# Five edits to a two-layer FP32 transformer kernel on one core: the squares a weight half later, a block-masked bias, an earlier third chunk, fewer unused matmuls, and the head norm on column groups

## The chip, the cores and the metric

The kernel runs on one core of one Trainium2 chip. The metric is the device time of one execution in microseconds. One execution was also recorded by the hardware profiler; all rows of a trace in this document come from such an execution, and its times count from the start of its span.

The core's engines are named as the trace names them: PE is the matrix engine (PEld is its weight load, which overlaps), DVE the vector engine, ACT the scalar engine, POOL the GpSimd engine, SP the engine that here only starts transfers. Each engine runs its own instructions in order and waits on semaphores for the others.

## The reference

Two transformer blocks follow each other on 256 tokens of width 1024, all in FP32. Cut to what matters here:

```python
def first_block(x, ...):
    proj = rms_norm(x, attn_norm_g) @ w_in
    y_moba = attention(rope(q), rope(k), v)          # 8 heads of 64, causal
    og = gla_attention(gq, gk, gv, log_a)            # 4 heads, 128 values each
    og = og * lax.rsqrt(jnp.mean(og * og, axis=-1, keepdims=True) + EPS) * gla_norm_g   # the head norm
    y_gla = og * silu(gr)
    x = x + concat(y_moba, y_gla) @ w_out
    h = causal_dwconv(rms_norm(x, ffn_norm_g) @ w_ffn_up, conv_w, conv_b)   # width 3
    x = x + (silu(h_gate) * h_val) @ w_ffn_down
    return rms_norm(x, final_norm_g)

def second_block(x, c, ...):
    (sh1, sc1, g1, sh2, sc2, g2, sh3, sc3, g3) = split(silu(c) @ w_ada + b_ada)
    x = x + 0.5 * g1 * swiglu(modulate(rmsnorm(x), sh1, sc1), ffn1_w_in, ffn1_w_out)
    z = modulate(rmsnorm(x), sh2, sc2) @ w_in        # latents, chunk attention q k v, two gates
    y_a = mla_attention(...) @ w_branch_a            # normalised latents, then w_uq and w_ukv
    y_b = chunk_attention(..., rel_bias) @ w_branch_b   # scores + rel_bias, masked by chunks of 64
    x = x + g2 * ((sigmoid(gate_a) * y_a + sigmoid(gate_b) * y_b) @ w_out)
    x = x + 0.5 * g3 * swiglu(modulate(rmsnorm(x), sh3, sc3), ffn2_w_in, ffn2_w_out)
    return rmsnorm(x, final_norm)
```

The feed-forward widths are 2816, so each up projection has 22 pairs of 128 columns and each down projection 22 tiles of contraction.

## The kernel before, in words

Activations stand with features on the 128 partitions and the 256 tokens along the free axis. Every product of an activation with a weight is done in three passes of FP32R matmuls (`three`, L393 to L395): weight-high by activation-high, weight-high by activation-low, weight-low by activation-high.

The weights come as 282 **halves** of 128 x 1024 (512 KB). A half is loaded by SP into one of four slots of `raw`, ACT copies it to `w_hi` (`hi`, L881), DVE subtracts to `w_lo` (`lo`, L1285), and PE uses it in 24 matmuls. Two halves are one **chunk**. SP may load half h when `w_lo` of half h-4 is made; ACT may write `w_hi` of half h when PE has used half h-4; PE waits for `lo_ready` before each half. All engines' orders are written out by hand.

The stages in order: input projection (chunks 0 to 11), its attention and gated linear attention between them, the output projection (12 to 15), the convolved up projection (16 to 37, halves 32 to 75), its down projection (halves 76 to 97), the second block's first up projection (98 to 141) and down projection (142 to 163), its input projection and latents (from half 164), eight gate chunks with the attentions between them, the branches, the output projection, the last up projection (halves 216 to 259) and the last down projection (260 to 281).

At a stage's first pair of chunks (`first_two`) PE takes the first halves of both chunks in turn, feature tile by feature tile, as the normalised tiles arrive. Before it, where the input isn't taken raw, `keep_clock` issues `IDLE_SPREAD` matmuls of 128 x 384 in FP32 whose output nobody reads; the trace shows two rows for each such matmul.

In `ffn_down`, output tile o is done by PE every 22 groups of three matmuls. DVE adds it to `X` (`ffn_resid`, L1389 or L1391) at the half that `OUT_AT` names, ACT squares it right then (`square`, L889; after the first block `gain_square`, L895, too), and POOL adds the squares up (L343, L351). PE sums them over partitions early in the next `first_two` (`sums`, at feature tile `sums_at`), since the next stage takes `X` unnormalised and scales its output.

In the convolved up projection ACT takes a chunk from PSUM with the middle tap (L993), then makes the `w_hi` of two chunks on; DVE adds the two other taps (L1546, L1549), frees the bank, makes the `w_lo`, and multiplies. While that goes on DVE also takes 72 dot products of `ada_w` with `silu(c)` (`ada`, L1576) in slots of its own.

The head norm (in the loop over g at g == 3) sums the squares of four heads by 8 matmuls with one moving column (L728), takes root and reciprocal of 128 x 8 values and spreads them back by 8 matmuls of 128 columns (L484). The bias of the chunk attention is loaded by POOL in one transfer (L373) and POOL adds the mask to it in eight instructions (L377), once the latents' root is taken (`lat_sd`).

## Time and profile before

| | |
|---|---|
| median of 3 runs | 881.8 us (881.03, 881.8, 885.49) |
| the profiled execution's own time | 885.38 us |
| its span in the trace | 883.6 us |
| PE busy | 864.9 us (98%), 7342 matmul rows |
| DVE busy | 702.6 us (80%) |
| ACT busy | 474.2 us (54%) |
| POOL busy | 88.7 us (10%) |
| weight matmuls, 128 x 256 and 128 x 258 | 6726 of the matmul rows, by the groups of L393 to L395, L467 to L469 and L796 to L798 |

Some 1.8 us of the profiled execution lie outside its span. A matmul's busy time in the trace (276 to 281 ns for 256 columns) is longer than the step from one to the next, since they are pipelined; so "98% busy" says that PE seldom waits, and not how fast it goes. The step is read from a count of matmuls over a stretch. An idle time in brackets behind a row is what the engine stood idle before that row, and what ended it.

### The profile page before, as it was taken

How to read it: one execution, taken by the hardware profiler on the slowest of the kernel's cores; microseconds unless marked ns; L12 is line 12 of the kernel's file. 1: busy time of each engine (PE TensorE's matmuls, PEld its weight loads, DVE VectorE, ACT ScalarE, POOL GpSimd, SP SyncE). 2: the span in 40 equal slices, each digit the busy share in tenths (PEclk: the TensorE clock that was granted, in tenths of full speed). 3: DMA queues.
4: the chain of work that ended last, by engine and by line, in shares of the span. 5: the costliest groups of instructions: out<-in, count | busy, mean ns of one | idle time of the engine just before them, and what ended most of it. 6: DMA issues, size and time to landing. Idle time of an engine off the chain costs nothing.

```text
span 883.6 us, 19377 instructions
## 1 busy us (share of the span) xinstructions
PE 864.9 (98%) x7342; PEld 838.6 (95%) x7342; DVE 702.6 (80%) x1109; ACT 474.2 (54%) x747; POOL 88.7 (10%) x135
## 2 busy tenths in 40 slices
PE   8999999999999999999999999999999999999996
PEld 7988998999999999999999999888899999999996
DVE  4998755889998788888887877888989998766552
ACT  4846665655555458444443467555645754444452
POOL 1022002000000321000001100300010100000010
PEclk8999999999999999999999999999999999999999
DMA  7543336556667985688888866655577568556651
GB/s 269 172 163 96 121 123 259 164 180 207 210 213 263 330 301 180 220 291 293 286 293 282 300 224 241 213 191 178 205 250 258 207 196 287 196 199 192 211 172 48
DMA packets 53335, 191.80 MB, mean 217 GB/s; under 512 B 5920, under 2 KB 6432, under 8 KB 53152
## 3 DMA queue, kind: packets, MB, share of 16 engines
q1 hardware_dynamic: 41760, 149.96, 50.9%
q0 software_dynamic: 10656, 39.33, 13.1%
q10 hardware_dynamic: 864, 1.73, 0.6%
q8 instruction: 39, 0.64, 0.3%
q14 instruction: 16, 0.13, 0.0%
HBM read 189.95 MB, written 1.05 MB: 216 GB/s over the span
## 4 chain that ended last, share of the span: by engine, by line
PE 84%; DVE 11%; ACT 3%; issue 1%; DMA 1%; SPq 0%; POOL 0%; DVEq 0%; ACTq 0%
PE ps L393 25%; PE ps L394 24%; PE ps L395 24%; DVE w_lo L1285 5%; DVE ada_raw L1576 2%; ACT w_hi L881 1%; PE ps L467 1%; PE ps L532 1%; PE ps L469 1%; PE ps L468 1%; PE ps L589 1%; DMA raw<-w 1%; PE ps L563 1%; PE ps L400 1%; PE ps L484 1%
## 5 line engine op out<-in xcount | busy, mean ns | idle before, releaser
L1285 DVE TENSOR_TENSOR w_lo<-raw,w_hi 128x1024 fp32r<-128x1024 f32 (+1 forms) x282 | 341.2, 1226 | 86.9 <-ACT w_hi L881 86.5
L393 PE MATMUL ps<-xh,w_hi 128*128 128x256 f32 x1296 | 364.6, 281 | 1.6 <-DVE w_lo L1285 1.6
L394 PE MATMUL ps<-xl,w_hi 128*128 128x256 f32 x1296 | 360.4, 278 | 0.0
L395 PE MATMUL ps<-xh,w_lo 128*128 128x256 f32 x1296 | 360.4, 278 | 0.0
L881 ACT ACTIVATE w_hi<-raw 128x1024 fp32r<-128x1024 f32 (+1 forms) x282 | 287.0, 1047 | 45.6 <-PE ps L395 30.0
L393 PEld LDWEIGHTS ps<-xh,w_hi 128*128 128x128 f32 x1296 | 244.1, 188 | 5.2 <-issue 3.4
L395 PEld LDWEIGHTS ps<-xh,w_lo 128*128 128x128 f32 x1296 | 244.9, 189 | 0.0
L394 PEld LDWEIGHTS ps<-xl,w_hi 128*128 128x128 f32 x1296 | 243.5, 188 | 0.9 <-issue 0.8
L393 PE MATMUL ps<-act_hi,w_hi 128*128 128x256 f32 x528 | 146.4, 277 | 1.5 <-DVE w_lo L1285 1.5
L395 PE MATMUL ps<-act_hi,w_lo 128*128 128x256 f32 x528 | 146.0, 277 | 0.0
L394 PE MATMUL ps<-act_lo,w_hi 128*128 128x256 f32 x528 | 146.0, 277 | 0.0
L393 PEld LDWEIGHTS ps<-act_hi,w_hi 128*128 128x128 f32 x528 | 99.1, 188 | 2.1 <-DVE w_lo L1285 1.9
L394 PEld LDWEIGHTS ps<-act_lo,w_hi 128*128 128x128 f32 x528 | 99.3, 188 | 0.0
L395 PEld LDWEIGHTS ps<-act_hi,w_lo 128*128 128x128 f32 x528 | 99.2, 188 | 0.0
L1576 DVE SCALAR_TENSOR_TENSOR ada_raw<-ada_raw,cact 128x1024 f32<-128x1024 f32 x72 | 87.5, 1218 | 0.0
L334 POOL DMA_DIRECT2D ada_raw<-ada_w x72 | 38.5, 535 | 452.1 <-DVE ada_raw L1576 452.1
L1000 ACT ACTIVATE sg<-ps 128x256 f32<-128x256 f32 x36 | 13.8, 384 | 115.2 <-PE ps L395 115.2
L889 ACT ACTIVATE xn<-X 128x256 f32<-128x256 f32 (+1 forms) x37 | 17.7, 479 | 84.0 <-DVE X L1391 50.3
L393 PE MATMUL ps<-xr_h,w_hi 128*128 128x258 f32 x176 | 50.6, 287 | 3.0 <-DVE w_lo L1285 3.0
L394 PE MATMUL ps<-xr_l,w_hi 128*128 128x258 f32 x176 | 50.0, 284 | 0.0
L993 ACT ACTIVATE cv<-ps,cols 128x256 f32<-128x256 f32 x44 | 22.5, 562 | 51.3 <-PE ps L395 51.3
L395 PE MATMUL ps<-xr_h,w_lo 128*128 128x258 f32 x176 | 49.7, 282 | 0.0
(261 smaller groups left out, 1144.5 us busy)
## 6 DMA issues: line engine op xcount, KB each, us to landing
raw<-w SPq DMA_DIRECT2D x282, 512.0 KB, 4.3
ada_raw<-ada_w POOLq DMA_DIRECT2D x72, 512.0 KB, 4.7
X<-x_in SPq DMA_DIRECT2D x4, 256.0 KB, 5.7
bm<-bias_in POOLq DMA_DIRECT2D x1, 1024.0 KB, 6.2
out<-X SPq DMA_DIRECT2D x4, 256.0 KB, 2.4
tab<-tab_in ACTq DMA_DIRECT2D x1, 640.0 KB, 4.4
gmask<-gmask_in ACTq DMA_DIRECT2D x1, 512.0 KB, 5.3
cact<-c_in POOLq DMA_DIRECT2D x1, 512.0 KB, 6.0
```

Source lines behind the costliest of these rows:

```text
L334: pool.dma_start(ada_raw[:, n % 4, :], ada_w[n, :, :]).then_inc(ada_landed[n % 4], 16)
L393: pe.matmul(o, lh, rh, start=start, stop=False, skip_group_check=True)
L394: pe.matmul(o, lh, rl, start=False, stop=False, skip_group_check=True)
L395: return pe.matmul(o, ll, rh, start=False, stop=stop, skip_group_check=True)
L400: pe.matmul(ps[:, bank, 0:3 * P], mean[:, 0, :], mean[:, :, :].rearrange("p a n -> p (a n)"), start=True, stop=True)
L467: pe.matmul(o, ah[:, kc, a], w_hi[:, slot(h), wcol], start=first and f == 0, stop=False, skip_group_check=True)
L881: f(w_hi[:, slot(h), 0:n], raw[:, slot(h), 0:n], ACT.Copy).then_inc(hi_ready, 1)
L889: f(xn[:, k:k + n, :], X[:, k:k + n, :], ACT.Square).then_inc(sq_done, n)
L993: ins = f(cv[:, v, t2, 0:S], ps[:, b, t2 * S:t2 * S + S], ACT.Identity, scale=wcol, bias=bcol)
L1000: f(sg[:, v, :], ps[:, b, 0:S], ACT.Silu).then_inc(sg_done, 1)
L1285: v.tensor_tensor(w_lo[:, slot(h), 0:n], raw[:, slot(h), 0:n], w_hi[:, slot(h), 0:n].bitcast(F32), ALU.subtract).then_inc(lo_ready, 1)
L1576: v.scalar_tensor_tensor(out=ada_raw[:, k, :], in0=ada_raw[:, k, :], scalar=1.0, in1=cact[:, :], op0=ALU.mult, op1=ALU.mult, accum_out=mod ...
```

## The change

- `IDLE_SPREAD` goes from 2 to 1 (the two `first_two` that don't take their input raw: the kernel's start and the convolved up projection).
- Head norm: the sums of squares are 4 matmuls with 32 stationary columns of 1/128 each, to 32 partitions per head (column groups), 256 moving columns; root and reciprocal are now of 128 x 256; the spread is 4 matmuls of 256 columns with a matrix `g_pick` that picks a head's row.
- The norm before the convolved up projection sums tile 6 first, then 0 and 1 (which wait for POOL's sum), then 7.
- Convolved up projection: the high and low parts of the third chunk's weights are made before the first chunk is taken from PSUM.
- `ffn_down`: each square stands one weight half later in ACT's order. DVE's order is as it was.
- Bias: the masked quarter is filled with -1e30 by a memset, the rest loaded by two transfers; the eight additions go. DVE waits for the transfers at the chunk attention's masks.
- Last up projection: POOL adds the squares only when the low parts of the first two halves are made, and PE sums them after the fourth feature tile, not the third.

```diff
@@ -28,7 +28,7 @@
 IDLE = 6
-IDLE_SPREAD = 2
+IDLE_SPREAD = 1
 NEXT = [(0, 1), (1, 1), (2, 2), (4, 2), (6, 2)]
@@ -152,7 +152,7 @@
                     ("pt1", [P, 2, 768], F32), ("st1", [P, 2, 3, 4], F32),
-                    ("g_rstd", [P, S], F32),
+                    ("g_rstd", [P, S], F32), ("g_pick", [P, 4, P], F32),
                     ("posi", [P, S], I32)])
@@ -172,7 +172,7 @@
         bank_free = [sem("bank0_free"), sem("bank1_free")]
-        mean_ready, consts_ready, pool_zero = sem("mean_ready"), sem("consts_ready"), sem("pool_zero")
+        pick_ready, mean_ready, consts_ready, pool_zero = sem("pick_ready"), sem("mean_ready"), sem("consts_ready"), sem("pool_zero")
         rstd_spread, out6_full = sem("rstd_spread"), sem("out6_full")
@@ -317,6 +317,11 @@
             pool.memset(b1["AT1"][:, :, :], 0.0).then_inc(pool_zero, 1)
+            own.mark(pool.memset(b1["g_pick"][:, :, :], 0.0))
+            own.wait()
+            for h in range(4):
+                pool.memset(b1["g_pick"][32 * h:32 * h + 1, h, :], 1.0).then_inc(pick_ready, 1)
+            pool.wait_ge(pick_ready, 4)
@@ -370,14 +375,12 @@
             pool.wait_ge(half_used, 2 * C_LAT)
-            pool.dma_start(b2["bm"][:, :, :], bias_in).then_inc(bias_landed, 16)
-            pool.wait_ge(lat_sd, 1)
-            pool.wait_ge(bias_landed, 16)
-            for h in range(8):
-                ins = pool.tensor_tensor(b2["bm"][:, h, :], b2["bm"][:, h, :], table("chunked", S), ALU.add)
-            ins.then_inc(bm_ready, 1)
+            pool.memset(b2["bm"][0:64, :, P + 64:S], NEG).then_inc(bm_ready, 1)
+            pool.dma_start(b2["bm"][0:64, :, 0:P + 64], bias_in[0:64, :, 0:P + 64]).then_inc(bias_landed, 16)
+            pool.dma_start(b2["bm"][64:P, :, :], bias_in[64:P, :, :]).then_inc(bias_landed, 16)
             for n in range(49, 68):
                 load_ada(n)
+            pool.wait_ge(lo_ready, 2 * C_UP[2] + 2)
             for k in (2, 4, 6):
@@ -502,10 +505,11 @@
-                pe.wait_ge(sq_sum, added)
                 for j, k in enumerate(tiles_left):
...
                         pe.wait_ge(sq_done, KC * q + k + 1)
+                    else:
+                        pe.wait_ge(sq_sum, added)
                     m = token_sums(k, j == 0, j == len(tiles_left) - 1)
@@ -592,7 +596,7 @@
                 raw_in = f > 0
-                first_two(c0, m_x, sums=sums, sums_at=f, shifted=raw_in)
+                first_two(c0, m_x, sums=sums, sums_at=2 * f - 1, shifted=raw_in)
                 n = 2
@@ -723,10 +727,9 @@
                     for h in range(4):
-                        pe.wait_ge(go_sq, 2)
-                        for t in range(2):
-                            m = pe.matmul(ps[:, 2, 2 * h + t:2 * h + t + 1], b1["g_sd"][:, h, t * P:t * P + P], mean[:, 2, 0:1],
-                                          start=h == 0 and t == 0, stop=True, skip_group_check=True)
+                        pe.wait_ge(go_sq, h // 2 + 1)
+                        m = pe.matmul(ps[32 * h:32 * h + 32, 2, 0:S], mean[:, 2, 0:32], b1["g_sd"][:, h, :], start=True, stop=True,
+                                      skip_group_check=True)
                     m.then_inc(go_ss, 1)
@@ -736,17 +739,17 @@
+                    pe.wait_ge(pick_ready, 4)
                     pe.wait_ge(go_rstd, 1)
...
                     for h in range(4):
-                        for t in range(2):
-                            o = (h % 2) * S + t * P
-                            m = spread(ps[:, 2 - 2 * (h // 2), o:o + P], b1["g_rstd"][:, 2 * h + t:2 * h + t + 1], h % 2 == 0 and t == 0)
+                        m = pe.matmul(ps[:, 2 - 2 * (h // 2), (h % 2) * S:(h % 2) * S + S], b1["g_pick"][:, h, :], b1["g_rstd"][:, :],
+                                      start=h % 2 == 0, stop=True, skip_group_check=True)
                         if h % 2:
...
             mix_ends(C_OUT1, b1["yh1"], b1["yl1"])
-            norm_tokens(1, 1, 2, (0, 1, 6, 7))
+            norm_tokens(1, 1, 2, (6, 0, 1, 7))
@@ -992,7 +995,8 @@
                     ins.then_inc(cv_base, 1)
-                    hi(c + 2, i=i)
+                    if j:
+                        hi(c + 2, i=i)
                     act.wait_ge(cv_gate, n)
@@ -1008,6 +1012,7 @@
+                hi(c0 + 2)
                 for j in range(2):
@@ -1034,12 +1039,12 @@
                     hi(c0 + p // 2, halves=(p % 2,))
-                    if p in OUT_AT:
-                        square(q, OUT_AT[p])
+                    if p - 1 in OUT_AT:
+                        square(q, OUT_AT[p - 1])
                         if fi == 0:
-                            gain_square(OUT_AT[p])
-                    if last and p in OUT_AT:
-                        final_gain(OUT_AT[p])
+                            gain_square(OUT_AT[p - 1])
+                        if last:
+                            final_gain(OUT_AT[p - 1])
                     if not last and p >= 17:
@@ -1130,7 +1135,7 @@
                     act.wait_ge(go_ss, 1)
-                    f(b1["g_rstd"][:, 0:8], ps[:, 2, 0:8], ACT.Sqrt, bias=epsc[:, 0:1]).then_inc(go_sd, 1)
+                    f(b1["g_rstd"][:, :], ps[:, 2, 0:S], ACT.Sqrt, bias=epsc[:, 0:1]).then_inc(go_sd, 1)
                 att_yh(g, yh1, g)
@@ -1548,11 +1553,13 @@
                         ins.then_inc(cv_gate if t2 == 0 else bank_free[b], 1)
-                    lo(c + 2, i=i, halves=(0,))
+                    if j:
+                        lo(c + 2, i=i, halves=(0,))
                     dve.wait_ge(bank_free[b], u // 2 + 1 + i)
...
                     v.tensor_tensor(av[:, vv, :], sg[:, vv, :], cv[:, vv, 1, 0:S], ALU.mult).then_inc(cv_own, 1)
-                    lo(c + 2, i=i, halves=(1,))
+                    if j:
+                        lo(c + 2, i=i, halves=(1,))
                     dve.wait_ge(cv_own, 3 * (j + 1) + 6 * i)
@@ -1578,6 +1585,7 @@
+                lo(c0 + 2)
                 for j in range(2):
@@ -1733,7 +1741,7 @@
                     dve.wait_ge(go_sd, 1)
-                    v.reciprocal(b1["g_rstd"][:, 0:8], b1["g_rstd"][:, 0:8]).then_inc(go_rstd, 1)
+                    v.reciprocal(b1["g_rstd"][:, :], b1["g_rstd"][:, :]).then_inc(go_rstd, 1)
                 att_y(g, yh1, yl1, g)
@@ -1857,6 +1865,7 @@
                     dve.wait_ge(bm_ready, 1)
+                    dve.wait_ge(bias_landed, 32)
                     att_mask(g, b2["sm2"], b2["st2"], 0.125, lambda a, b_: b2["bm"][:, h:h + 2, a:b_])
             mask2(4)
```

How instructions move, three places. Lines of the changed kernel are 3 and more further down: its L884 is `hi` (L881 before), L892 the square (L889), L898 the gain square (L895), L996 and L1001 are L993 and L997.

ACT from the end of the norm into the convolved up projection, before (`cact` belongs to the ada products, `cv` is the chunk taken from PSUM, `sg` its gate):

```order
L1160 ACTIVATE cact<-cact 128x1024
L993 ACTIVATE cv<-ps,cols 128x256 x2
L881 ACTIVATE w_hi<-raw 128x1024 x2
L997 ACTIVATE sg<-cv 128x256
L993 ACTIVATE cv<-ps,cols 128x256 x2
L881 ACTIVATE w_hi<-raw 128x1024 x2
```

and after:

```order
L1165 ACTIVATE cact<-cact 128x1024
L884 ACTIVATE w_hi<-raw 128x1024 x2
L996 ACTIVATE cv<-ps,cols 128x256 x2
L1001 ACTIVATE sg<-cv 128x256
L996 ACTIVATE cv<-ps,cols 128x256 x2
L884 ACTIVATE w_hi<-raw 128x1024 x2
```

The two halves of the third chunk stand ahead of the first chunk's `cv`; DVE's two `w_lo` move in the same way.

ACT in the middle of the first block's down projection, before (each `xn<-X` is a square, which waits for DVE's addition to `X`):

```order
L881 ACTIVATE w_hi<-raw 128x1024 x3
L889 ACTIVATE xn<-X 128x256
L895 ACTIVATE gain_sq<-X,cols 128x256
L881 ACTIVATE w_hi<-raw 128x1024
L907 ACT_TABLE_LOAD
L907 ACTIVATE epsc<-epsc 128x1
L881 ACTIVATE w_hi<-raw 128x1024
L889 ACTIVATE xn<-X 128x256
L895 ACTIVATE gain_sq<-X,cols 128x256
```

and after:

```order
L884 ACTIVATE w_hi<-raw 128x1024 x3
L892 ACTIVATE xn<-X 128x256
L898 ACTIVATE gain_sq<-X,cols 128x256
L910 ACT_TABLE_LOAD
L910 ACTIVATE epsc<-epsc 128x1
L884 ACTIVATE w_hi<-raw 128x1024 x2
L892 ACTIVATE xn<-X 128x256
L898 ACTIVATE gain_sq<-X,cols 128x256
```

The half that stood behind each square now stands ahead of it.

POOL around the bias (`bm`), before (the first `xn` row is the second block's sum of squares, the last one that of the last norm):

```order
L343 TENSOR_TENSOR xn<-xn 128x256 x2
L373 DMA bm<-bias_in 128x2048
L377 TENSOR_TENSOR bm<-bm,tab 128x256 x8
L334 DMA ada_raw<-ada_w 128x1024 x19
L343 TENSOR_TENSOR xn<-xn 128x512 x3
```

and after:

```order
L348 TENSOR_TENSOR xn<-xn 128x256 x2
L378 MEMSET bm 64x8x64
L379 DMA bm<-bias_in 64x8x192
L380 DMA bm<-bias_in 64x2048
L339 DMA ada_raw<-ada_w 128x1024 x19
L348 TENSOR_TENSOR xn<-xn 128x512 x3
```

The eight additions are gone, and the loads behind them no longer wait for `lat_sd`.

## Rows read from the trace of the kernel before

**Rows 1.** The chain that ended last, share of the span by engine.
```profile
PE 84%; DVE 11%; ACT 3%; issue 1%; DMA 1%; SPq 0%; POOL 0%; DVEq 0%; ACTq 0%
```

**Rows 2.** PE's waits, whole run: waiting <- waited for: us in total, times, longest.
```profile
PE ps L393 <- DVE w_lo L1285: 6.1, 7, 1.4
```

**Rows 3.** Busy time and counts by stretch: span, busy (x) per engine, PEclk, DMA, GB/s.
```profile
160.00:270.00 110.00, 110.00 (x936) 110.00 (x936) 99.43 (x185) 62.26 (x97) 2.11 (x4) 1.00 0.65 204
365.00:475.00 110.00, 110.00 (x973) 110.00 (x973) 93.26 (x141) 45.03 (x58) 11.09 (x21) 1.00 0.84 283
```

**Rows 4.** Timeline at the convolution's third chunk: start, us, engine, line, out<-in [idle before].
```profile
156.15 0.86 DVE L1549 SCALAR_TENSOR_TENSOR cv<-ps,cols,cv 128x254 f32<-128x254 f32 x2
...
156.93 1.22 DVE L1285 TENSOR_TENSOR w_lo<-raw,w_hi 128x1024 fp32r<-128x1024 f32 x1
...
158.20 0.39 PE L393 MATMUL ps<-xh,w_hi 128*128 128x256 f32 x1 [1.21 <-DVE w_lo L1285]
```

**Rows 5.** Timeline in the first down projection, output tile 3.
```profile
307.47 0.42 DVE L1389 TENSOR_TENSOR X<-ps,X 128x256 f32<-128x256 f32 x1
...
308.42 0.74 POOL L343 TENSOR_TENSOR xn<-xn 128x256 f32<-128x256 f32 x1 [2.51 <-ACT xn L889]
...
308.64 2.94 ACT L881 ACTIVATE w_hi<-raw 128x1024 fp32r<-128x1024 f32 x3
...
309.72 1.23 DVE L1285 TENSOR_TENSOR w_lo<-raw,w_hi 128x1024 fp32r<-128x1024 f32 x1 [1.84 <-ACT w_hi L881]
```

**Rows 6.** PE's timeline, the matmul that ends each wait in or behind the down projections.
```profile
311.00 0.38 PE L393 MATMUL ps<-act_hi,w_hi 128*128 128x256 f32 x1 [0.94 <-DVE w_lo L1285]
...
333.79 0.36 PE L393 MATMUL ps<-xr_h,w_hi 128*128 128x258 f32 x1 [0.74 <-DVE w_lo L1285]
...
494.65 0.38 PE L393 MATMUL ps<-act_hi,w_hi 128*128 128x256 f32 x1 [0.59 <-DVE w_lo L1285]
...
518.12 0.36 PE L393 MATMUL ps<-xr_h,w_hi 128*128 128x258 f32 x1 [0.85 <-DVE w_lo L1285]
```

**Rows 7.** Timeline at the latents: POOL's mask additions, DVE, and PE's first matmul behind.
```profile
552.58 6.18 POOL L377 TENSOR_TENSOR bm<-bm,tab 128x256 f32<-128x256 f32 x8 [14.87 <-ACT l_sd L1203]
...
555.91 2.25 DVE L1820 SCALAR_TENSOR_TENSOR lat<-lat,cols,l_sd 128x256 f32<-128x256 f32 x3
558.08 1.76 DVE L1285 TENSOR_TENSOR w_lo<-raw,w_hi 128x1024 fp32r<-128x1024 f32 x1
...
561.94 0.35 PE L393 MATMUL ps<-cqh,w_hi 128*128 128x256 f32 x1 [1.28 <-issue]
```

**Rows 8.** Timeline ahead of the last up projection.
```profile
690.23 1.49 POOL L343 TENSOR_TENSOR xn<-xn 128x512 f32<-128x512 f32 x1 [7.81 <-ACT xn L889]
...
690.49 2.32 DVE L1285 TENSOR_TENSOR w_lo<-raw,w_hi 128x1024 fp32r<-128x1024 f32 x1
...
693.07 0.36 PE L393 MATMUL ps<-xr_h,w_hi 128*128 128x258 f32 x1 [1.37 <-DVE w_lo L1285]
```

**Rows 9.** Busy time in that up projection's raw chunks, columns as in rows 3.
```profile
699.00:718.00 19.00, 19.00 (x160) 19.00 (x160) 18.13 (x25) 16.63 (x26) 0.00 (x0) 1.00 0.47 152
```

**Rows 10.** Timeline at the norm before the convolved up projection.
```profile
143.32 2.77 PE L400 MATMUL ps<-mean 128*128 128x384 f32 x4
...
144.53 0.43 DVE L1317 TENSOR_TENSOR xl<-xn,xh 128x256 fp32r<-128x256 f32 x1
```

**Rows 11.** The stretch of those matmuls, columns as in rows 3.
```profile
142.60:145.90 3.30, 3.30 (x9) 2.09 (x9) 2.25 (x6) 1.45 (x4) 0.13 (x1) 0.50 0.79 288
```

**Rows 12.** Timeline at the head norm, and one output copied out behind it.
```profile
112.37 1.84 PE L728 MATMUL ps<-mean,g_sd 128*128 128x1 f32 x16
...
115.49 0.42 DVE L1489 TENSOR_TENSOR yl<-ps,yh 128x256 fp32r<-128x256 f32 x1 [0.74 <-ACT yh L971]
```

**Rows 13.** Groups by shape: four concurrent 32-column tiles, and a reciprocal of 128 x 256.
```profile
L670 PE MATMUL ps<-xn,w_glr 128*32 128x256 f32 x16 | 1.1, 385 | 0.0
L1290 DVE RECIPROCAL rstd_x<-sd 128x256 f32<-128x256 f32 x1 | 1.7, 1746 | 0.0
```

## The prediction

> **What bounds the kernel now.** I read the chain that ended last first: PE holds 84% of it and DVE 11% [rows 1]. So PE sets the end, and a change is worth what it takes from PE's waits, from PE's work, or from the step between its matmuls. The second view is who waited for whom: PE's first matmul of a half waited 7 times for `w_lo`, 6.1 us in all [rows 2]. The third is a count of matmuls over a stretch, because a busy PE need not be a fast one. In the convolved up projection 936 matmuls started in 110 us, in the second block's up projection 973 [rows 3]: a step of 117.5 ns against 113.1 ns, both at full granted clock and both without a wait. I call them the long and the short step. The change doesn't name them, but a wait removed may change which one follows. The last view is the timeline at each wait, to see what was late there.
>
> An idle time in a row counts from a matmul's modelled end, and a matmul lasts 0.28 us where the step is 0.12 us; so a wait costs its idle time plus about 0.16 us.
>
> **The third chunk's weights first.** PE stood idle 1.21 us for the `w_lo` of the third chunk, 1.37 us lost, because DVE made it (start 156.93) behind the first chunk's taps [rows 4]. Both copies now stand ahead of the first chunk's evacuation, on ACT and on DVE. What is late next is the bank: the third chunk writes where the first stood, and DVE's last tap, which frees it, ends at 156.15 + 0.86 = 157.01. PE would come at 158.20 - 1.37 = 156.83 and waits some 0.2 us for the bank. I take 1.15 us. Nothing else is behind the moved copies but the evacuation, which waits for PE's end of the first chunk anyway.
>
> **The square one half later.** At output tile 3 of the first down projection DVE adds to X at 307.47, ACT squares, squares with the gain, and only then starts the next `w_hi` (308.64); DVE idles 1.84 us for it [rows 5], and PE then idles 0.94 us: 1.10 us lost [rows 6]. The high part could have been made at once, since its raw half had long landed and its slot was free. DVE gains 1.84 us per output tile. But POOL's two additions (0.74 us each, one in rows 5) fell into that idle time, and now fall on busy DVE. Rows 8 show what that may cost: an addition of 1.49 us beside a `w_lo` that took 2.32 us where others take 1.23 us [rows 5]. So the collision costs DVE between nothing and POOL's whole 1.48 us; I take the latter, a net 0.36 us per tile. Four tiles (0 to 3) stand before the wait, 1.4 us, which is more than the 1.10 us that was missing: this wait goes. Behind the down projection PE loses 0.74 + 0.16 = 0.90 us in the same way [rows 6]; there the sums of the last tile follow close behind, and I take 0.75 us. The second block's down projection has the same two waits, 0.75 and 1.01 us [rows 6], and only one addition per tile: 1.75 us. Together 3.6 us; from 2.0 (the collisions take back the waits in the middle) to 3.8.
>
> The Trainium skill ("SBUF — State Buffer", Who interferes with whom) says that a DVE instruction with two SBUF inputs and a GpSimd instruction that reads SBUF block each other for the whole instruction. Rows 8 agree, 2.32 us against 1.23 us. By that rule the upper price above is the one to take.
>
> **The bias without additions.** POOL's eight additions run from 552.58 for 6.18 us. In that time DVE's three instructions on the latents took 2.25 us, where two of this kind take 0.86 us [rows 4], so three 1.3 us; and the `w_lo` behind took 1.76 us [rows 7] against 1.23 us. That is 0.95 + 0.53 = 1.5 us on DVE ahead of PE's first matmul on them, which stood idle 1.28 us, 1.44 us lost [rows 7]. With the additions gone the whole wait goes, 1.4 us; if DVE's slowness had another source, nothing. The transfers are one more, on POOL's queue, and their data is wanted 40 us later.
>
> **The last up projection.** PE idled 1.37 us for that 2.32 us `w_lo` [rows 8]. POOL now waits for it, so it takes 1.23 us and PE starts 1.1 us earlier. But POOL's three additions start at 691.7, not at 690.23: their 4.5 us now lie wholly on DVE's X and weight parts, and DVE comes out of them up to 1.0 us later than now. PE's sums also stand a feature tile later. Behind them DVE is busy 18.13 of 19 us [rows 9], so it can't catch up, and PE, which is 1.1 us earlier, meets it. I keep 0.3 us of 1.1; the bounds are -0.3 and 1.1.
>
> **Norm, fewer unused matmuls, head norm.** Before the convolved up projection four rows of unused matmuls begin at 143.32 and take 0.64 us each, at half clock (0.50, rows 11), so they end at 145.88; the first tile of `xl` is ready at 144.96 [rows 10]. With two rows PE can start at 145.0, 0.88 us earlier. The new order of the sums saves PE some 0.27 us of waiting for POOL. Head norm: the sums took 1.84 us [rows 12]; the gate's 16 rows in four column groups take 1.1 us [rows 13], so 8 rows 0.55 us and a bit, 1.1 us saved. The reciprocal now takes 1.75 us [rows 13], where one of 8 columns was short; it delays the `yl` behind it, which began at 115.49 [rows 12], by nothing in clock time but against a PE that is 1.1 us earlier, so PE waits 0.7 us. I take 0.4 us (bounds -0.5 and 1.1). At the kernel's start I take 0.2 us of what the norm gives, since DVE paces what follows. That is 0.2 + 0.4 + 0.27 + 0.88 = 1.75 us; but real matmuls that start at 144.1 run at 1.2 GHz until the clock rises at about 146, so half of it is lost. I take 0.8 us.
>
> **The sum.** 1.15 + 3.6 + 1.4 + 0.3 + 0.8 = 7.25 us, rounded to 7.3. Against the profiled execution's own 885.4 us (span 883.6 and 1.8 outside) that is 878.1. Now the step: in the convolved up projection some 1,010 matmuls ran behind the wait at 158.20, and each took 4.5 ns more than the short step [rows 3], 4.5 us in all. The three unprofiled runs are 881.0, 881.8 and 885.5: two of them 4 us shorter than the profiled one, the third like it. I read that as this stretch at one step or the other. The median of before is then one with the short step, and so is my forecast: 881.8 - 7.3 = 874.5 us. A half per cent is 4.4 us and about what a measurement of this kernel can tell from no change; the line for faster is 877.4.
>
> **The rivals.**
> - *The long step stays in that stretch.* The 0.2 us wait for the bank starts PE anew there, as the longer wait did, and which step follows a wait differs from one to the next: after 311.00 and 494.65 [rows 6] PE went on fast, after 158.20 slowly. For it: the profiled run. Against it: two of three other runs. Time: 885.4 - 7.3 = 878.1, with smaller gains 879.
> - *DVE gives it back.* The collisions cost more than the waits did in both down projections, and the last up projection gives nothing. Then 3.6 becomes 1.0 or so and 0.3 becomes 0: 881.8 - 7.3 + 2.9 = 877.4, say 878. For it: DVE is at 99.43 of 110 us in one up projection [rows 3]. Against it: in the down projections it idles 1.84 us per tile.
> - *The clock stays low.* The unused matmuls stand where PE has just been at 0.50 [rows 11]. With half of them gone the clock may rise later. If it stayed low as long again as in that row, 3.3 us would hold only 1.65 us of work, and so at each of the two places: 874.5 + 2 to 3 = 877. The Trainium skill ("TensorE: Matmul & The Clock Gate", What's actually happening) says that activity releases the throttle, which speaks for keeping them. The trace agrees in that the rise comes after these matmuls. Against it: real matmuls take their place 0.4 us later.
> - *Slower.* The short step is lost where PE has it now. The stretches from 337 to 494 and from 698 to 875 hold some 1,370 and 1,550 matmuls at 113.1 ns; at 117.5 ns they cost 6.1 and 7.0 us. If the stalls removed before them leave PE in the long step there, the time is 885.4 - 7.3 + 13.1 = 891. It decides from about 1,650 such matmuls on (7.3 us / 4.4 ns). Against it: both stretches begin with matmuls of 258 columns, after which it was the short step each time.
>
> **How the numbers follow.** Forecast 874.5 with the short step: 0.53. Long step, 878.1 to 879: 0.22. DVE gives it back, 878: 0.13. Low clock, 877: 0.07. Slower, 891, or something like it: 0.05. Faster than 877.4 are 0.95 of the first, 0.3 of the second, 0.4 of the third and 0.6 of the fourth, 0.66; slower than 886.2 are 0.04; the rest is 0.30. The forecast's own terms are uncertain by +-2 us, 872 to 877. The range takes in the second and third cases with their errors: 871.5 to 880.5.
>
> **What would show it.** In the profile after: PE's waits for `w_lo` fall from 7 to 2 or fewer. The wait near 157 is 0.3 us or less and names a tap of DVE or nothing. No row of a `w_hi` behind a square has DVE waiting 1.8 us. A POOL addition stands beside a `w_lo` or an ada product of 1.9 us or more in the first down projection. The three latent instructions take 1.3 us and the wait at 561 is gone. In the last up projection the `w_lo` that took 2.32 us takes 1.2, and PE waits somewhere from 700 to 717 for DVE. Counts over 110 us in the convolved up projection say 973 or 936. The forecast is wrong if these counts rise and the time doesn't fall, or if the waits go and come back elsewhere on PE in the same size.

## The result and the profile after

The changed kernel took 878.5 us (median of 20 runs, 871.0 to 884.3) where the kernel before took 881.8 us (20 runs, 879.9 to 885.5): a ratio of 0.9941, interval 0.9921 to 0.996. The ratio compares means and leaves out the 884.3 us run as a slow one (877.3 for 882.4 us); by the medians it is 0.9963. The median is inside the predicted range and 4 us above the predicted 874.5 us. The spread is the news: 13 us, where the kernel before has 6. The profiled execution took 871.0 us (span 869.2), 14.4 us less than the profiled one of before.

The chain that ended last, answering to [rows 1], and PE's waits in the changed kernel, answering to [rows 2] (waiting <- waited for: us in total, times, longest):

```profile
PE 88%; DVE 8%; ACT 1%; issue 1%; DMA 1%; SPq 0%; DVEq 0%; ACTq 0%
```
```profile
PE ps L396 <- DVE w_lo L1290: 0.9, 2, 0.5
...
PE ps L396 <- DVE xl L1357: 0.7, 1, 0.7
...
PE ps L396 <- DVE xl L1322: 0.6, 2, 0.3
PE ps L396 <- DVE act_lo L1575: 0.4, 1, 0.4
PE ps L396 <- DVE yl L1494: 0.3, 1, 0.3
PE ps L396 <- DVE cv L1554: 0.2, 1, 0.2
```

The waits for `w_lo` fell from seven to two. The wait for `xl` of L1357 is the longest single one that is new among the weight matmuls.

Counts over fixed stretches of the changed kernel, answering to [rows 3]: the convolved up projection, and a stretch of the last up projection:

```profile
158.00:268.00 110.00, 110.00 (x973) 110.00 (x972) 102.10 (x189) 65.05 (x101) 2.12 (x4) 1.00 0.68 207
...
720.00:830.00 110.00, 110.00 (x973) 110.00 (x972) 73.91 (x107) 50.04 (x65) 4.43 (x5) 1.00 0.66 212
```

In this execution the convolved up projection had the short step: 973 matmuls in 110 us, 936 before.

The third chunk [rows 4], DVE's and PE's timelines (start, us, engine, line, operation, [idle before <- releaser]):

```profile
154.05 0.86 DVE L1554 SCALAR_TENSOR_TENSOR cv<-ps,cols,cv 128x254 f32<-128x254 f32 x2
```
```profile
155.05 0.38 PE L396 MATMUL ps<-xh,w_hi 128*128 128x256 f32 x1 [0.16 <-DVE cv L1554]
```

The wait for the weights (1.21 us) has become one of 0.16 us for DVE's last tap, which frees the bank, as forecast.

The first down projection [rows 5, 6], POOL and DVE:

```profile
297.51 1.20 POOL L348 TENSOR_TENSOR xn<-xn 128x256 f32<-128x256 f32 x1 [2.14 <-ACT xn L892]
298.67 1.71 POOL L356 TENSOR_TENSOR gain_sq<-gain_sq 128x256 f32<-128x256 f32 x1
```
```profile
296.89 1.22 DVE L1290 TENSOR_TENSOR w_lo<-raw,w_hi 128x1024 fp32r<-128x1024 f32 x1
298.02 1.77 DVE L1583 SCALAR_TENSOR_TENSOR ada_raw<-ada_raw,cact 128x1024 f32<-128x1024 f32 x1
...
299.72 1.75 DVE L1290 TENSOR_TENSOR w_lo<-raw,w_hi 128x1024 fp32r<-128x1024 f32 x1
```

DVE no longer waits behind a square, and the collisions are there: 1.77 and 1.75 us beside POOL's additions, 1.22 us alone: 1.08 us for the tile where the forecast took 1.48, and none of the 1.9 us or more that it named as a sign. POOL pays too, 1.71 us for an addition of 0.74 us [rows 5]. The Trainium skill ("SBUF — State Buffer", Who interferes with whom) has the one blocking the other for whole instructions, which these rows agree with. PE doesn't wait: no row of `w_lo` stands ahead of PE there.

The latents [rows 7], DVE:

```profile
543.76 1.28 DVE L1828 SCALAR_TENSOR_TENSOR lat<-lat,cols,l_sd 128x256 f32<-128x256 f32 x3
...
544.95 1.22 DVE L1290 TENSOR_TENSOR w_lo<-raw,w_hi 128x1024 fp32r<-128x1024 f32 x1
```

2.25 and 1.76 us have become 1.28 and 1.22, and PE's wait of 1.28 us is gone.

The last up projection [rows 8, 9], all engines:

```profile
676.13 1.22 DVE L1290 TENSOR_TENSOR w_lo<-raw,w_hi 128x1024 fp32r<-128x1024 f32 x1
...
677.43 2.73 POOL L348 TENSOR_TENSOR xn<-xn 128x512 f32<-128x512 f32 x2 [8.93 <-DVE w_lo L1290]
...
677.60 0.36 PE L396 MATMUL ps<-xr_h,w_hi 128*128 128x258 f32 x1 [0.45 <-DVE w_lo L1290]
...
678.05 2.39 DVE L1337 SCALAR_TENSOR_TENSOR xr_l<-X,modA,xr_h 128x256 fp32r<-128x256 f32 x2
...
702.80 0.38 PE L396 MATMUL ps<-xh,w_hi 128*128 128x256 f32 x1 [0.72 <-DVE xl L1357]
```

The `w_lo` is down to 1.22 us; now the two `xr_l` beside POOL take 2.39 us where such a pair took 0.87. DVE doesn't catch up, and PE stands idle 0.72 us for it at 702.80: start to start 1.01 us. Of all the new waits this one cost the most, as the runs below show.

The norm and the head norm [rows 10 to 13], PE and DVE, and the granted clock (third number from the end of a row) in two executions of the changed kernel, the first and the one called a_again:

```profile
141.65 1.49 PE L403 MATMUL ps<-mean 128*128 128x384 f32 x2
...
143.44 0.55 PE L396 MATMUL ps<-xh,w_hi 128*128 128x256 f32 x1 [0.29 <-DVE xl L1322]
```
```profile
112.32 0.64 PE L731 MATMUL ps<-g_sd,mean 128*32 128x256 f32 x8
...
113.54 1.75 DVE L1744 RECIPROCAL g_rstd<-g_rstd 128x256 f32<-128x256 f32 x1 [3.77 <-ACT g_rstd L1138]
```
```profile
115.62 0.38 PE L396 MATMUL ps<-yh,w_hi 128*128 128x256 f32 x1 [0.27 <-DVE yl L1494]
```
```profile
141.00:144.00 3.00, 2.71 (x8) 1.59 (x8) 2.01 (x6) 1.15 (x3) 0.17 (x1) 0.50 0.84 243
144.00:147.00 3.00, 3.00 (x27) 3.00 (x27) 3.00 (x8) 1.66 (x3) 0.00 (x0) 0.98 0.99 401
```
```profile
143.00:149.00 6.00, 5.54 (x26) 5.57 (x27) 5.90 (x12) 3.85 (x6) 0.00 (x0) 0.50 1.01 389
```

The head sums cost 0.64 us for 1.84, the reciprocal 1.75 us as estimated, and PE waits 0.27 us idle for the `yl` behind it. The clock rose at 144.1 in the first execution and only behind 149 in the second.

### The profile page after: what moved, and what is told of

Same layout as the page of the kernel before. It is cut to its first block, busy times and chain, and to the rows that moved or that the text cites. A ratio compares the mean times of both kernels' runs of the same rounds, so it can differ in the third digit from the quotient of the medians.

```text
span 869.2 us, 19335 instructions
## 1 busy us (share of the span) xinstructions
PE 854.4 (98%) x7322; PEld 828.0 (95%) x7322; DVE 708.6 (82%) x1109; ACT 477.6 (55%) x747; POOL 101.4 (12%) x134
## 3 DMA queue, kind: packets, MB, share of 16 engines
HBM read 189.82 MB, written 1.05 MB: 220 GB/s over the span
## 4 chain that ended last, share of the span: by engine, by line
PE 88%; DVE 8%; ACT 1%; issue 1%; DMA 1%; SPq 0%; DVEq 0%; ACTq 0%
PE ps L396 26%; PE ps L397 26%; PE ps L398 26%; DVE w_lo L1290 2%; PE ps L470 1%; PE ps L472 1%; PE ps L471 1%; PE ps L536 1%; PE ps L593 1%; DMA raw<-w 1%; PE ps L567 1%; DVE ada_raw L1583 1%; PE ps L553 0%; PE ps L575 0%; PE ps L543 0%
## 5 line engine op out<-in xcount | busy, mean ns | idle before, releaser
L884 ACT ACTIVATE w_hi<-raw 128x1024 fp32r<-128x1024 f32 (+1 forms) x282 | 288.7, 1050 | 89.8 <-PE ps L398 63.2
L1583 DVE SCALAR_TENSOR_TENSOR ada_raw<-ada_raw,cact 128x1024 f32<-128x1024 f32 x72 | 91.4, 1272 | 0.4 <-DMA ada_raw<-ada_w 0.4
L348 POOL TENSOR_TENSOR xn<-xn 128x256 f32<-128x256 f32 (+1 forms) x24 | 32.7, 1364 | 208.7 <-ACT xn L892 199.5
L996 ACT ACTIVATE cv<-ps,cols 128x256 f32<-128x256 f32 x44 | 22.5, 562 | 44.5 <-PE ps L398 44.5
```

The lines of the kernel that those rows point to most:

```text
L348: pool.tensor_tensor(xn[:, 0:n, :], xn[:, 0:n, :], xn[:, k:k + n, :], ALU.add).then_inc(sq_sum, 1)
L884: f(w_hi[:, slot(h), 0:n], raw[:, slot(h), 0:n], ACT.Copy).then_inc(hi_ready, 1)
L996: ins = f(cv[:, v, t2, 0:S], ps[:, b, t2 * S:t2 * S + S], ACT.Identity, scale=wcol, bias=bcol)
L1583: v.scalar_tensor_tensor(out=ada_raw[:, k, :], in0=ada_raw[:, k, :], scalar=1.0, in1=cact[:, :], op0=ALU.mult, op1=ALU.mult, accum_out=mod ...
```

## The experiments

All profiles have the same 6,726 weight matmuls (six of them have 512 columns), so a stretch can be timed from one matmul's start to another's whatever stands between. Stretches that matter, in us (in a the clock differs, in b, c and d the step). Stretch a begins with the first output projection's 25th matmul, b with the third chunk's first, c behind PE's wait for `act_lo`, and d behind its wait near 702 us or in the same place where there is none:

```
                                     n  before changed a_again u_last u_idle u_squares b_plain n_flip s_after s_best
a to the conv.'s third chunk       264   38.62   36.41   38.41  37.82  35.90     37.69   36.81  35.53   36.32  36.67
b convolved up projection         1010  119.06  114.58  119.05 119.05 119.05    119.06  119.06 114.73  114.74 114.82
c first down pr., behind its wait  498   59.61   57.48   59.56  57.48  57.48     59.80   57.48  57.61   57.63  57.66
  second up and down projection   1572  183.16  180.33  180.34 180.33 180.34    183.15  180.33 180.34  180.33 180.33
  last up projection's start       192   24.10   25.20   25.22  24.09  25.30     25.21   24.08  24.08   24.96  24.09
d the rest, to the last matmul    1391  157.67  157.75  157.75 157.67 163.93    163.93  157.67 157.67  157.99 157.67
```

**a_again: the changed kernel once more.** No edit.

> The changed kernel once more, unchanged. Theory A (the step between PE's weight matmuls is 113.3 or 117.8 ns, taken when PE starts after an interruption, and kept until the next one; which of the two differs from one execution to the next): runs spread over 10 us or more again, 871 to 884; in the profile, the waits are those of the first profile within 0.3 us each, and the time differs from 871.0 by 4.5 ns for each matmul that has changed from the short step to the long one (4.6 us for the convolved up projection's 1012, 2.2 us for the first down projection's 496), within 0.7 us. Theory B (the spread comes from transfers or from waits that come and go): the sum of PE's waits differs between the two profiles by as much as the time does, and the steps are the same.

Six runs, 871.95 to 880.14, median 873.9; the profiled one took 880.14 us, 9.1 more than the first. Its convolved up projection and first down projection were long,

```profile
160.00:270.00 110.00, 110.00 (x936) 110.00 (x935) 98.58 (x182) 62.25 (x97) 2.11 (x4) 1.00 0.65 196
```

which is 4.47 + 2.08 us (b and c), less 0.45 us that PE now didn't wait for `act_lo`. The clock ahead of the convolution (a, with 0.5 us of the first output projection the other way) gave 2.0, the kernel's start 0.8. Theory A holds for the steps; that the clock would add 2.8 us was not in it. Theory B falls: the waits at the third chunk and at 702 us are the same within 0.1 us.

**n258 and n256: one unused matmul into running streams.** They are fp32, with the means' matrix on both sides.

```
+ def nudge(): pe.matmul(ps[:, 3, 0:258], mean[:, 0, :], mean[...][:, 0:258], start=True, stop=True)
+ nudge()   # behind the conv.'s third chunk; in each down projection behind its first 8 tiles (n256: 256)
```

> The changed kernel with one unused matmul of 258 columns put into the running stream of weight matmuls at four places: behind the third chunk of the convolved up projection (48 matmuls after it starts) and after 24 matmuls of each of the three down projections. Theory A1 (a matmul of 258 columns shifts the stream into the short step, as it seemed to behind the two up projections that begin with such columns): short step (113.3 ns) in the profile behind each of the four, runs at 871.5 to 875 with a spread under 5 us, median 873.5, since only stretches in the attention stages still vary. Theory A2 (the step is settled at the start of a stretch, nothing inside it changes it): runs as those of the unchanged kernel, median 879, spread over 10 us, and a profile with the long step on both sides of a 258-column matmul in at least one of the four if it is there at all. Theory A3 (any odd matmul throws the dice again): median 877 to 879, with stretches that change their step at the inserted matmul in either direction.

> The same with 256 columns in the four inserted matmuls. Theory A1: the count of columns matters, so nothing changes, median 879 with a spread over 10 us. Theory A2: the same. Theory A3 (any odd matmul): a step may change at the inserted matmul; median 877 to 879. If this kernel is as short as the one with 258 columns (under 875), it is the insertion and not its column count.

874.5 us (six runs, 873.3 to 878.8) and 876.9 us (seven, 875.1 to 878.4). Neither told the theories apart: in all eight places of the two profiles the stream was short ahead of the inserted matmul and stayed short. The first down projection was long in n256 all the same (59.56 us), since the wait for `act_lo` stands behind the insertion, and there PE starts anew.

**u_ahead: three parts undone.**

```
- IDLE_SPREAD = 1                         + IDLE_SPREAD = 2
- sums_at=2 * f - 1                       + sums_at=f
- pool.wait_ge(lo_ready, 2 * C_UP[2] + 2)
- conv_up: hi(c0 + 2), lo(c0 + 2) first   + both behind the first chunk's evacuation
```

> The changed kernel with three of its parts undone, at three places that don't meet: the third chunk's weights back behind the first chunk's evacuation, four unused matmuls ahead of the convolved up projection in place of two (two in the other stages where this number counts), and in the last up projection the sums one feature tile earlier and POOL's additions without their wait. By the prediction's terms: the third chunk's wait is back at 1.37 us idle and more (+1.15 us), the first tile of the convolution starts 0.4 to 0.9 us later (+0.44), and in the last up projection the w_lo of 2.3 us and PE's wait of 1.37 us for it come back, while the waits of 0.29 and 1.01 us behind it go (+0.3 in all). So 1.9 us over the changed kernel at equal steps. The rival (these parts gain nothing, since what they remove comes back elsewhere): within 0.5 us at equal steps. On the steps: if the wait of 1.4 us at the third chunk makes the long step likelier there, more than half of the executions are above 879; if not, the spread is that of the changed kernel.

The runs were not longer but shorter, 873.0 us (six runs, 871.8 to 876.3) for 878.5. At equal steps, which is what was forecast, it is otherwise: this profile and the changed kernel's first are both short in b, c and d, and it took 872.2 us for 871.0, 1.2 us longer and not 1.9. The wait at the third chunk is back,

```profile
156.32 0.39 PE L395 MATMUL ps<-xh,w_hi 128*128 128x256 f32 x1 [1.21 <-DVE w_lo L1287]
```

1.49 us start to start against 0.44: 1.05 us for this part. Stretch a is 0.35 us longer beyond that, with the unused matmuls back (0.44 was forecast). But the last up projection's start took 24.73 us for 25.20, with no wait between the columns of 258 and the rest.

**n_sizes: other column counts.** fp32 matmuls of 256, 128, 254, 258 and 260 columns in the second output projection, one of 258 at the latents.

> The changed kernel with single unused matmuls put into two streams of weight matmuls that had the long step (117.8 ns) in all profiles so far. In the latents' stage one of 258 columns after 48 matmuls. In the second output projection, each 24 matmuls behind the one before and from its 72nd on: 256 columns, 128, 254, 258, 260. Theory A1 (258 columns shift the stream into the short step): the latents' stage goes on at 113.3 ns behind its inserted matmul (0.3 us less), the projection is long behind 256 and 128 and short behind 258 (the last 48 matmuls, 0.2 us less). Theory A2 (settled when PE starts behind an interruption, and nothing inside changes it): 117.8 ns throughout in both. Theory A3 (any inserted matmul throws again): changes in either direction, behind 256 and 128 as often as behind 258.

One run, 874.7 us. Inconclusive: both streams were short from their start, and all six insertions left them short. That both had been long in all profiles, as the expectation has it, was a misreading: the matmuls around the latents' insertion were short in every profile, and the last 144 of the second output projection were short in three of the six so far.

**u_last, u_idle, u_squares: the parts one by one.**

```
u_last:    - sums_at=2 * f - 1    + sums_at=f      - pool.wait_ge(lo_ready, 2 * C_UP[2] + 2)
u_idle:    - IDLE_SPREAD = 1      + IDLE_SPREAD = 2
u_squares: - if p - 1 in OUT_AT:  + if p in OUT_AT:    and POOL's eight mask additions again
```

> The changed kernel with only the last up projection's part undone: POOL adds the squares without waiting for the third chunk's w_lo, and the sums of squares stand one feature tile earlier (behind the first tile of the second block's up projection's start as well as of the third's). By the prediction's term (the wait was worth +0.3 us): 0.3 us longer at equal steps, with the w_lo at 2.3 us again and PE's wait for it at 1.37 us. By what the kernel with three parts undone showed (24.73 us against 25.20 us from the third up projection's first matmul to its 192nd): 0.5 us shorter than the changed kernel at equal steps, PE's waits of 0.29 and 1.01 us behind it gone, and the wait for w_lo no longer than in the changed kernel.

> The changed kernel with four unused matmuls ahead of the convolved up projection again (and two for one at the other stages). Theory C (the granted clock rises some time after PE is busy again without a gap, and the fewer unused matmuls leave a gap that can put the rise off): from the fall near 142 us the clock is at 0.50 for 3.0 to 3.3 us in every profile, and the first 96 weight matmuls of the convolution take 12.9 us or less, where three profiles with two unused matmuls had 11.6, 12.1 and 13.0 and one had 14.1 us; median of the runs no higher than the changed kernel's, highest of them lower. Theory D (the length of the low stretch differs from one execution to the next whatever stands there): a low stretch over 4 us may come here too; the median is 0.4 to 0.9 us above the changed kernel's.

> The changed kernel with two parts undone: the squares of the three down projections right behind their output tile's weight half as before, and the bias mask by POOL's eight additions again. By the prediction: waits of 1.1 us and 0.9 us come back in the first down projection (net 1.85), 0.75 and 1.0 us in the second (1.75), 1.4 us at the latents; 5.0 us longer than the changed kernel at equal steps, 3.4 us at least. The rival (these waits came from elsewhere and are not undone by it): under 2 us. And if more interruptions mean shorter stretches of one step, the runs spread less: 6 us or less, where the changed kernel's spread is 10 or more.

*u_last*: 874.5 us (six runs, 870.3 to 876.9). From the second output projection's last 144 matmuls to the end it took 199.29 us for 199.98 (17.53 + 24.09 + 157.67 for 17.03 + 25.20 + 157.75): undoing this part gains 0.7 us. PE waits once, ahead of the columns of 258, and nowhere behind:

```profile
683.79 0.36 PE L395 MATMUL ps<-xr_h,w_hi 128*128 128x258 f32 x1 [0.94 <-DVE w_lo L1289]
```

The `w_lo` of 2.3 us did not come back (1.21 us), against the first expectation, and PE's wait for it grew from 0.45 to 0.94 us idle, against the second.

*u_idle*: 878.8 us (12 runs, 876.6 to 884.3). Its clock did not fall at all ahead of the convolution. Its last stretch is the first one seen long behind the wait near 702:

```profile
706.32 0.38 PE L396 MATMUL ps<-xh,w_hi 128*128 128x256 f32 x1 [0.83 <-DVE xl L1357]
```
```profile
720.00:830.00 110.00, 110.00 (x937) 110.00 (x936) 73.91 (x109) 45.52 (x60) 3.05 (x4) 1.00 0.65 208
```

937 matmuls for 973, 6.2 us over the stretch. So the unused matmuls can't be judged by this median, and it decides nothing between theories C and D.

*u_squares*: 882.1 us (12 runs, 878.7 to 889.0), as long as the kernel before (ratio 1.0002, 0.9972 to 1.0031). The waits are back,

```profile
308.39 0.38 PE L399 MATMUL ps<-act_hi,w_hi 128*128 128x256 f32 x1 [1.14 <-DVE w_lo L1293]
...
331.18 0.36 PE L399 MATMUL ps<-xr_h,w_hi 128*128 128x258 f32 x1 [0.74 <-DVE w_lo L1293]
...
559.29 0.36 PE L399 MATMUL ps<-cqh,w_hi 128*128 128x256 f32 x1 [1.28 <-issue]
```

with two more in the second block: start to start less a step, 1.30 + 0.90 + 0.74 + 1.01 = 3.95 us for the squares and 1.44 for the mask, 5.4 us where 5.0 were forecast. The medians are 3.6 us apart. The spread did not shrink (10 us): it also has the wait near 702, and its last stretch was long too.

**b_plain and n_flip.** b_plain is the changed kernel with the edits of u_last and u_idle together. n_flip is b_plain with inserted matmuls of the weights' own type:

```
+ def nudge(v, bank, cols=258, n=1):  # one pass, v is xh, act_hi or yh2
+     pe.matmul(ps[:, bank, 0:cols], v[:, 0, 0:128], v[:, 0:2, :][..][:, 0:cols], start=True, stop=True)
+ chunk(c0 + 2, halves=(0,)); nudge(xh); chunk(c0 + 2, halves=(1,))
+ if t == FT and f == 0: nudge(act_hi)      # first down projection, behind its wait
+ branch products, every 24: 258; six of 258; 256; fp32 256; fp32 258; fp32 384
```

> The changed kernel with the last up projection's part undone (POOL doesn't wait, the sums one feature tile earlier) and four unused matmuls ahead of the convolution again. Theory A (a wait inside the third up projection, behind its columns of 258, throws the step of the 1391 matmuls behind it, and without that wait they have the short step each time): no interruption between the first 258-column matmul and the end of the last down projection, 157.7 us for these 1391 in the profile, no run above 879, median 873 to 875. Theory B (the step of that stretch differs from one execution to the next anyway): one run in four or so at 880 to 884, as in the changed kernel. On the clock: theory C (with four unused matmuls the low stretch ahead of the convolution is 3.3 us at most), against D (6.4 us at times here too, as in four of seven profiles with two of them).

> The same kernel with single unused matmuls in running streams, of the weights' own type (one pass, 258 columns) behind the first half of the convolution's third chunk (24 matmuls behind the place where PE is interrupted) and behind the last four feature tiles' wait in the first down projection (12 matmuls behind it). In the branch products ahead of the second output projection (192 matmuls, which had the long step in all ten profiles so far), each 24 matmuls behind the last: one of 258 columns, six of 258, one of 256, then fp32 ones (four passes) of 256, 258 and 384. Theory A1 (columns of 258 bring the short step): the convolved up projection (1010 matmuls) and the first down projection (498) are short in the profile, 114.5 and 57.5 us, whatever they are ahead of the inserted matmul; in the branch products the step changes to 113.3 ns behind the one or the six of 258 columns; median 872.5, highest run 876. Theory A2 (only an interruption throws the step): branch products long throughout, the two stretches long or short as they come, median as the kernel without inserted matmuls plus 0.7 us (its own time, 1.2 us for all of them, less what lies in waits). Theory A4 (it is the four-pass type that brings it): the branch products turn short only behind the fp32 ones.

*b_plain*: 871.3 us (four runs, 870.4 to 875.0), ratio 0.9884 (0.986 to 0.9908). *n_flip*: 872.4 us (five, 871.0 to 873.3), with 1.9 us for its tests. Mean step of the eight matmuls ahead of each insertion and of eight behind it (from the seventh on), in ns, from the starts in the profiles:

```
n_flip   branch products, 258      117.9 -> 113.4     s_after  convolution, 258          113.4 -> 113.4
n_flip   branch products, 6 x 258  113.4 -> 113.4     s_after  first down pr., 258       113.8 -> 113.4
n_flip   branch products, 256      113.4 -> 117.8     s_after  behind 702.8 us, 258      117.8 -> 113.2
n_flip   branch pr., fp32 256      117.8 -> 117.8     s_best   convolution, 258          117.8 -> 113.4
n_flip   branch pr., fp32 258      117.8 -> 113.4     s_best   first down pr., 258       117.8 -> 113.4
n_flip   branch pr., fp32 384      113.4 -> 113.4     s_best   latents, 258              117.8 -> 117.6
n_flip   convolution, 258          113.4 -> 113.4     s_best   branch products, 258      117.9 -> 117.8
n_flip   first down pr., 258       113.4 -> 113.2     s_best   gate, 2nd output pr.      short, stay short
```

So a matmul inside a stream can change its step, and A2 falls. Behind a single one-pass matmul of 258 columns a long stream turned short four times of six, and a short one stayed short in all seven cases (one with six of them); the one of 256 columns made a short stream long. A1 holds mostly, not always. That the count of columns matters, and not any insertion, rests on the one case of 256 columns: with n258, n256 and n_sizes, 22 of 23 insertions of any kind into a short stream left it short.

**s_after: the changed kernel with only its three long stretches steered.** Three matmuls were inserted, not four as the expectation says.

```
+ if f != 1: chunk(c0 + n, halves=(0,)); nudge(xh); chunk(c0 + n, halves=(1,)); chunk(c0 + n + 1); n += 2
+ if t == FT and f == 0: nudge(act_hi)
```

> The changed kernel as it is, with four single unused matmuls of 258 columns (one pass, some 0.11 us each): 24 matmuls behind the places where PE is interrupted at the third chunk of the convolved up projection and in the third up projection (its wait near 702 us), 12 behind the wait in the first down projection. Theory A (its runs spread over 13 us because each of these interruptions leaves the next 1010, 498 and 1391 matmuls with the step of 113.3 or of 117.8 ns, 4.5, 2.2 and 6.3 us apart): all three stretches are short in the profile, whatever they are ahead of the inserted matmul, all waits stay as they are, runs within 871 to 876 (what is left is the clock ahead of the convolution, 2 us, and short stretches, 1.5 us), median 873 where the unchanged kernel has 878.5 in its first 20 runs. Theory B (the spread has another source, and the long step in some profiles is a result of it): median 877 to 879, highest run above 880.

873.1 us (six runs, 871.2 to 874.0), ratio 0.9891 (0.9862 to 0.9919): no run above 874.0, where the unchanged kernel had 17 of 26 above that. The wait is still there, and the step behind it was long for 24 matmuls:

```profile
702.79 0.38 PE L396 MATMUL ps<-xh,w_hi 128*128 128x256 f32 x1 [0.46 <-DVE xl L1370]
```
```profile
705.73 0.28 PE L407 MATMUL ps<-xh 128*128 128x258 f32 x1
```
```profile
720.00:830.00 110.00, 110.00 (x973) 110.00 (x972) 73.90 (x106) 50.24 (x66) 4.54 (x5) 1.00 0.65 213
```

Behind the inserted matmul 973 fit in 110 us. Theory B, with a median of 877 to 879 us, is ruled out. One reservation: these runs are from another chip than those of a_again. The kernel before, run beside them there, took 880.0 to 886.0 us, as elsewhere, but the changed kernel itself was not run on it.

**s_best: what gained, together.** b_plain, six insertions of 258 columns, and the last head's y ahead of the reciprocal:

```
- dve.wait_ge(go_sd, 1); v.reciprocal(g_rstd); att_y(g)    + att_y(g); dve.wait_ge(go_sd, 1); v.reciprocal(g_rstd)
```

> All that gained, put together: the changed kernel without the last up projection's part and with four unused matmuls ahead of the convolution (median 871.3 of four runs), with single unused matmuls of 258 columns in the output gate's, convolution's, first down projection's, latents', branch and second output projection's stretches, and with the last head's y on DVE ahead of the reciprocal. By theory A each of them is short behind its insertion: against the kernel with 258 columns and the branch tests (872.4 us) 1.9 us for the tests' own matmuls, 0.7 for the branch products, 0.4 for the latents; and PE's wait of 0.55 us near 114 us goes (0.4). That is 869.0 us, 867.5 to 871.5; if the inserted matmuls do nothing beyond the big stretches, 871.

870.65 us (six runs, 870.03 to 870.89), ratio 0.9861 (0.9833 to 0.9888): 10 us below the runs of before beside it (880.7) and 8 below the changed kernel's 878.5, with a spread of 0.9 us. PE's wait for `yl` is gone: 4.40 us for 4.94 from the first output projection's first matmul to its 25th. Forecast was 869.0; the latents and branch products kept the long step (1.1 us), so their insertions only cost; the other 0.5 us stay open.

## Why the prediction was right, and where it was off

The terms, against what undoing them or the table shows:

```
                          predicted   measured
third chunk first            1.15      1.05   (u_ahead)
squares one half later       3.6       3.95   (u_squares)
mask by blocks               1.4       1.44   (u_squares)
last up projection           0.3      -0.7    (u_last)
head norm                    0.4       0.8    (up to a: 52.69 + 4.63 us became 51.59 + 4.94)
norm, unused matmuls         1.15      1.5 or -0.5   (a: 2.2 less, or 0.2, of which 0.75 are step; u_ahead: 0.35)
start                        0.2      -0.4    (the 97th weight matmul starts at 29.63 us for 29.27; 28.87 to 30.32 elsewhere)
  these three, half kept     0.8       1.9 in the first profile, -1.0 in a_again
```

- **What bounds, and the waits.** Right. PE sets the end, and the six waits that 6.15 us of the forecast rested on went, or shrank, as worked out.
- **The collisions.** Their verdict was right: DVE had the time in the down projections. The price was too high, 1.48 us a tile for 1.08 in the rows above (1.77 and 1.75 us for twice 1.22).
- **The last up projection.** The forecast said that DVE would come out up to 1.0 us later, that PE would meet it between 700 and 717, and kept 0.3 of 1.1 us. PE met it at 702.80 and it took all of the gain and 0.7 us more.
- **The step that failed: the short step taken for granted.** "The median of before is then one with the short step, and so is my forecast" covered one stretch of 1,010. The slower rival named the last 1,550 matmuls too, 7.0 us, and was put at 0.05, since "both stretches begin with matmuls of 258 columns". True of before; but the wait that the forecast itself expected near 700 to 717 falls between those columns and the rest, and PE starts anew behind it. With that wait the stretch was long at its start in 3 of 8 profiles (u_idle, u_squares, s_after), in the six without it never, and no run of the five changed kernels without it was above 876.9 us. The two halves stood side by side and were not joined.
- **What was luck.** That the median lies in the range is in part luck. It is where the rival with the long step stood (878.1 to 879), and the convolved up projection began with that step in six of the twelve profiles that have the earlier third chunk; but three stretches vary, the runs lie from 871.0 to 884.3 us, and which stretches were long in the runs at the median is not known. Nor was it ever shown that the shorter runs of before (13 of 20 at 879.9 to 882.5 us, the others at 884.1 to 885.5) had the short step there; the 4 us between the groups fit, but its one profile is from a long run.
- **The clock.** The rival priced a second low stretch at 2 to 3 us for both places; the one ahead of the convolution cost 1.3 to 2.0. It came in four of eight profiles with two unused matmuls (6.8 us at 0.50 where the others have 3.4, added up from the clock in each microsecond) and in none of six with four (3.4 us or none). That is too few to call the cause shown.

With the step steered and nothing else, the changed kernel is at 873.1 us, 5.4 below its median. This fits the forecast of 874.5 as a price of the waits; the missing 4 us are then the step, and what the clock adds to them no run separates.

## What to carry to other kernels

Where PE runs one kind of matmul for 100 us, count matmuls over a fixed stretch before pricing waits, and in more than one profile. Ask of every wait, also a new one of half a microsecond, what uninterrupted stretch stands behind it: here one idle of 0.7 us put 6.2 us at stake. And a median of runs with 13 us of spread says little of one edit; undo it and time the same matmuls against each other.

## What the hardware showed that was not expected

- The start-to-start time of these weight-load-and-matmul pairs (fp32r, 128 x 128 by 256 columns, full clock) has two values, 113.3 and 117.8 ns, each kept for up to 1,400 matmuls. The Trainium skill ("TensorE: Matmul & The Clock Gate", Back-to-back issue gap) has a formula for an isolated matmul, N / 2.4 + 2.5 ns, by which 256 columns are an estimated 109.2 ns; both values of these traces are above it. Why there are two was not found.
- A hold too short to be listed as idle can change the step. In the second down projection of the kernel before a `w_lo` ended at 502.82 (start 501.59, 1.23 us), just late, and PE's next two starts are 160 ns apart:

```profile
502.94 0.32 PE L393 MATMUL ps<-act_hi,w_hi 128*128 128x256 f32 x1
503.10 0.28 PE L394 MATMUL ps<-act_lo,w_hi 128*128 128x256 f32 x1
```

  The step ahead of it was 113.3 ns and behind it 117.8 ns for 118 matmuls, 0.5 us; the profile of u_squares has the same in the same place. With the square a half later the stream was short throughout in all 12 other profiles, a gain that no term of the forecast held.
- Behind a one-pass matmul of 258 columns the short step followed in every case where it was short before, and four times of six where it was long; behind the up projections' runs of such columns with no wait between, in all profiles.
- An inserted fp32 matmul of 258 columns lengthened its stream by 0.45 us (n258: 158.21 us for 157.75 in d, 1 insertion), the one-pass one by 0.13 to 0.16 (stretches b and c of n_flip and s_after).
